# Recurrent gates on TensorE: one product for both neighbour tiles, from a tile that DMAs assemble

## The chip, the cores and the metric

The kernel runs on one core of a Trainium2 chip. The time is that of the device in microseconds; the kernel before took 1741.39 us (median of three runs, 1741.05 to 1741.88).

## What is computed

Two networks in a row on 256 tokens of width 1024: two layers with feed-forward blocks, a recurrent mixer (layer 0) or a pooling mixer (layer 1) and an embedding gate, then two layers with attention and a gated linear recurrence. The change touches only the gates of the recurrent mixer:

```python
xc = conv_b + sum(conv_w[k] * shifted(xb, k))            # 256 tokens x 1280 channels
xh = xc.reshape(B, S, 16, 80)                            # 16 heads of 80 channels
r  = sigmoid(einsum('bshi,hij->bshj', xh, w_a) + b_a)    # each head has its own 80 x 80 matrix
ig = sigmoid(einsum('bshi,hij->bshj', xh, w_x) + b_x)
a  = exp(-8 * r * softplus(-a_param))
h  = scan of a * h + sqrt(1 - a*a) * (ig * xc);  y = h * gelu(gate_branch);  out = y @ w_out
```

## The kernel before

It is one program with a hand-written order on each engine. Weights come in 1 MB blocks on SyncE's queue (L286) into a ring of three; ScalarE copies each block to its rounded part `hi` (L455), VectorE makes the rest `lo` (L927), and TensorE multiplies with both. This "split" of a block stands at the head of each iteration of a stage on ScalarE and VectorE, two blocks ahead of TensorE.

The recurrent mixer ("lru") has ten iterations of input projection, i = 0 to 9. In i = 0 to 4 TensorE makes the recurrent branch, two tiles of 128 channels each time. VectorE takes them out of PSUM (L1396) and convolves them (`convolve`, two instructions of L1406 and six of L1410 for two tiles); each tile that is finished adds 1 to `xc_ready`. So tiles 0 to 9 of `xc` exist in pairs, tiles 8 and 9 last.

The gates come in two groups, g = 0 and 1, of five tiles (640 channels, eight heads) each. Heads of 80 don't end where tiles of 128 end, so an output tile m of a group takes input from tiles m - 1, m and m + 1. `band` holds the heads' matrices as 128 x 128 blocks around the diagonal, zero elsewhere: 2 gates x 2 groups x 5 tiles x 384 columns. POOL clears it at the start (L337) and 48 small DMAs fill it (L356). For each output tile and each gate, TensorE makes two fp32 products at the ends of a group and three inside it (L2168), 13 for each group and gate. Group 0 follows the projection of i = 5 (called `half`), group 1 that of i = 6. Before a group TensorE waits for all of its five tiles of `xc`.

Both gates of the tile `ft` (0 to 9) go to bank `ft % 4` of psD. ScalarE applies the two sigmoids to it (L672, L673), each of which adds 1 to `gates_ready`, and from ft = 4 on TensorE waits until the bank's last reader is done: `gates_ready >= 2 * (ft - 3)` (L2164). So ft = 4 wants both sigmoids of ft = 0, and ft = 9 those of ft = 5.

ScalarE's order around this is, for i = 5: split of block 7, sigmoids of group 0, tanh of group 0 (L680); for i = 6: split of block 8, exp (L686) and sqrt (L688) of group 0, gelu of the first four gate tiles (L693), sigmoids of group 1; for i = 7: the next split, tanh of group 1 and so on. A function of another set than the last one needs a table load ahead of it, which has the line of its activation. The waits of `split` beyond one are semaphore instructions of their own (L449).

Of the kernel before, what the change touches and what calls it, by code (L numbers as in the profile page):

```python
# [25 lines left out]
P = 128  # L26
S = 256
# [4 lines left out]
R = 1280  # L32
RT = R // P
HD = 80
GT = 5
# [26 lines left out]
L_XC = L_XB + RT * (S + 3) + 2  # L62
L_GELU = L_XC + RT * S
L_IG = L_GELU + RT * S
BAND = L_IG + RT * S
POOL_M, POOL_B, POOL_S = 4096, 6144, 7168
Z, Q_B, V_B, A_QK, A_V, G_B, GATE_A, GATE_B = 2048, 4096, 5120, 6144, 8192, 9216, 10240, 12288
LOGF, TMP, KK = 14336, 16384, 18432
# [4 lines left out]
QK_T = GATE_B  # L73
SQUARES, TURNER = 22016, 22528
SCRATCH = 22784
assert BAND + 2 * 2 * GT * 384 <= SCRATCH


def head_pieces():
# [12 lines left out]
def build(nc, a, out):  # L92
# [5 lines left out]
    def sem(name):  # L98
        return ctx.enter_context(nc.semaphore(name))

    with ctx:
# [12 lines left out]
        scr = sb("scr", [P, SCRATCH])  # L114
# [13 lines left out]
        psD = ctx.enter_context(nc.psum_tensor("psD", [P, 4, 512], F32))  # L128
# [20 lines left out]
        first_landed, early_landed = sem("first_landed"), [sem(f"early_landed{i}") for i in range(2)]  # L149
        consts_loaded, gain_loaded = sem("consts_loaded"), sem("gain_loaded")  # L150
        band_zeroed, band_loaded = sem("band_zeroed"), sem("band_loaded")
        p_loaded, pool_loaded, mix_loaded = sem("p_loaded"), sem("pool_loaded"), sem("mix_loaded")
        param_loaded, param_turned = sem("param_loaded"), sem("param_turned")
        ident_loaded, first_gain_loaded, gains_loaded, gains_turned, gains_ready = sem("ident_loaded"), sem("first_gain_loaded"), sem("gains_loaded"), sem("gains_turned"), sem("gains_ready")
# [178 lines left out]

        @block.gpsimd
        def _(pool):
            band = view(BAND, 2, 2, GT, 384)
            pool.memset(scr[:, BAND:BAND + 2 * 2 * GT * 384], 0.0).then_inc(band_zeroed, 1)  # L337
            pool.dma_start(param_rows[0:4 * RT, :], a["lru_conv_w"][0].rearrange("k (f p) -> (k f) p", p=P)).then_inc(param_loaded, 16)
            for i, v in enumerate((a["lru_conv_b"], a["lru_b_a"], a["lru_b_x"], a["lru_a_param"])):
                pool.dma_start(param_rows[(4 + i) * RT:(5 + i) * RT, :], v[0].rearrange("(f p) -> f p", p=P)).then_inc(param_loaded, 16)  # L340
            for l in range(2):
                for e in range(2):
                    at = 8 * RT + (2 * l + e) * HEADS
                    pool.dma_start(param_rows[at:at + HEADS, :], a["hg_lb_logits_2"][e, l, :].rearrange("(f p) -> f p", p=P)).then_inc(param_loaded, 16)
            for i, g in enumerate(gains[1:]):
                pool.dma_start(gain_rows[1][i * KT:(i + 1) * KT, :], g.rearrange("(k p) -> k p", p=P)).then_inc(gains_loaded, 16)
            for t_, src in ((level_words, a["c_level"]), (rope_in[:], a["c_freq"]),
                            (pos_i[:], a["positions_2"].rearrange("b (t p) -> p (b t)", p=P))):
                pool.dma_start(t_, src, allow_slow_non_contiguous=True).then_inc(consts_loaded, 16)
            pool.wait_ge(band_zeroed, 1)  # L350
            pool.wait_ge(hi_ready, RAW + 2)
            for m, w in enumerate((a["lru_w_a"][0], a["lru_w_x"][0])):
                for head, row, tile, part, cnt in head_pieces():
                    col = head * HD - (tile - 1) * P
                    for g in range(2):
                        pool.dma_start(band[part:part + cnt, m, g, tile, col:col + HD],  # L356
                                       w[8 * g + head, row:row + cnt, :]).then_inc(band_loaded, 16)
            if row_gains:
                pool.dma_start(gain[:], row_gains[0].rearrange("(o d) -> o d", o=1).broadcast_to([P, D])).then_inc(gain_loaded, 16)
            rescaled = updates = 0  # L360
            for stage, nxt in zip(plan, plan[1:] + [("end",)]):
                kind = stage[0]
                if kind == "renorm":

                    pool.wait_ge(gain_loaded, 16 * (rescaled + 1))
                    for i, (t, c) in enumerate(BY_COLUMNS):
                        pool.wait_ge(h_ready, 2 * T * updates + i + 1)
                        cs = slice(512 * c, 512 * (c + 1))
                        pool.tensor_tensor(xn[:, t, cs], h[:, t, cs], gain[:, cs], ALU.mult).then_inc(hg_ready, 1)
                    rescaled += 1  # L370
                    if rescaled < len(row_gains):
                        pool.wait_ge(hg_ready, 2 * T * rescaled)
                        pool.dma_start(gain[:], row_gains[rescaled].rearrange("(o d) -> o d", o=1).broadcast_to([P, D])).then_inc(gain_loaded, 16)
                if kind == "pool":

                    pool.wait_ge(pool_loaded, 48)
                    pool.tensor_tensor(view(POOL_B, D), view(POOL_B, D), view(POOL_S, D), ALU.mult).then_inc(rows_biased, 1)
                if kind in ("ffn", "lru", "pool", "ple", "mix", "renorm", "rescale"):
                    updates += 1
                if kind == "lru":  # L380
                    pool.wait_ge(h_ready, 2 * T * (updates + 1))
                    pool.dma_start(view(POOL_M, T, 4, S), a["c_pool"]).then_inc(pool_loaded, 16)
                    pool.dma_start(view(POOL_B, D), a["pool_b"].broadcast_to([P, D])).then_inc(pool_loaded, 16)
                    pool.dma_start(view(POOL_S, D), a["pool_scale"].broadcast_to([P, D])).then_inc(pool_loaded, 16)
                if kind == "lru" or kind == "ple" and stage[2] == 0:
                    i = 0 if kind == "lru" else 1
                    pool.wait_ge(h_ready, 2 * T * (updates + 1))
                    pool.dma_start(view(PTOK, T, S), a["p"][i].rearrange("b (t p) d -> p (b t) d", p=P)).then_inc(p_loaded, 16)
                if kind == "lru" or kind == "mix" and stage[1] == 0:
                    l = 0 if kind == "lru" else 1  # L390
                    pool.wait_ge(h_ready, 2 * T * (updates + 1))
                    pool.dma_start(view(NRM_DA, 512), a["da_norm_2"][l].rearrange("(o d) -> o d", o=1).broadcast_to([P, 512])).then_inc(mix_loaded, 16)
                    pool.dma_start(view(NRM_HG, 512), a["hg_norm_2"][l].rearrange("(o d) -> o d", o=1).broadcast_to([P, 512])).then_inc(mix_loaded, 16)
                    pool.dma_start(view(LAM, 256), a["da_lambda_2"][l].rearrange("(o i) d -> o (i d)", o=1).broadcast_to([P, 256])).then_inc(mix_loaded, 16)
# [36 lines left out]
        def _(act):  # L431
# [133 lines left out]
            for stage, nxt in zip(plan, plan[1:] + [("end",)]):  # L565
# [98 lines left out]
                if kind == "lru":  # L664
                    half = R // FC
                    gelu = view(L_GELU, RT, S)
                    r, ig, th = view(L_R, RT, S), view(L_IG, RT, S), view(L_XB, RT, S)

                    def recurrent_gates(g):
                        for ft in range(g * GT, (g + 1) * GT):  # L670
                            act.wait_ge(gates_done, ft + 1)
                            act.activation(r[:, ft, :], psD[:, ft % 4, 0:S], ACT.Sigmoid, bias=lru_c[:, 1, ft:ft + 1]).then_inc(gates_ready, 1)  # L672
                            act.activation(ig[:, ft, :], psD[:, ft % 4, S:2 * S], ACT.Sigmoid, bias=lru_c[:, 2, ft:ft + 1]).then_inc(gates_ready, 1)  # L673
# [21 lines left out]
                    for i in range(2 * half):  # L695
# [6 lines left out]
                            recurrent_decay(1)  # L702
                        n += 1
                        if i == half:
                            recurrent_gates(0)
                            half_tanh(0)
                        if i == half + 1:
                            recurrent_decay(0)
# [1057 lines left out]
        def _(pe):  # L1766
# [293 lines left out]
            for stage, nxt in zip(plan, plan[1:] + [("end",)]):  # L2060
# [92 lines left out]
                    st["ffn"] += 1  # L2153
                if kind == "lru":
                    half = R // FC
                    band, xc = view(BAND, 2, 2, GT, 384), view(L_XC, RT, S)

                    def recurrent_gates(g):

                        pe.wait_ge(xc_ready, GT * (g + 1))  # L2160
                        for m in range(GT):
                            ft = g * GT + m
                            if ft >= 4:
                                pe.wait_ge(gates_ready, 2 * (ft - 3))  # L2164
                            for e in range(2):
                                ks = [k for k in (m - 1, m, m + 1) if 0 <= k < GT]
                                for k in ks:
                                    last = pe.matmul(psD[:, ft % 4, e * S:(e + 1) * S], band[:, e, g, k, (m - k + 1) * P:(m - k + 2) * P],  # L2168
                                                     xc[:, g * GT + k, :], start=(k == ks[0]), stop=(k == ks[-1]))
                            last.then_inc(gates_done, 1)  # L2170

                    for i in range(2 * half):
# [240 lines left out]
```

## Time and profile before

| | |
|---|---|
| median of the runs | 1741.39 us |
| profiled execution, time | 1741.45 us |
| profiled execution, span | 1739.6 us |
| TensorE busy (matmuls) | 1728.8 us, 99% |
| VectorE busy | 1262.9 us, 73% |
| ScalarE busy | 1003.7 us, 58% |
| DMA | 311.65 MB, mean 179 GB/s |

The span is the time from the first to the last instruction of the profiled execution; its time is measured around it. Busy shares are means over the whole span and over stages with different limits, so a change in a stretch of 30 us is read in the rows of that stretch. All times in the timelines are microseconds from the start of the span. The recurrent gates lie between 231 and 260 us.

### The profile page before, as it was taken

The numbers are of one execution on the slowest core, as the hardware profiler recorded it, in microseconds if no ns is written. First come the engines' busy times: TensorE is split into PE (matmuls) and PEld (weight loads), VectorE is DVE, ScalarE is ACT, GpSimd is POOL, SyncE is SP. The second block draws the span as 40 slices with busy tenths as digits, with TensorE's granted clock in tenths as the row PEclk, the third lists the DMA queues.
The fourth block names the chain that finished last, engine by engine and source line by source line (L and its number), as shares of the span: only waits on it lengthen the run. The fifth ranks groups of instructions, "written<-read, shape, count | busy, mean of one in ns | idle before, by whom it ended". The sixth has DMA issues, their size and how long they took to land.

```text
span 1739.6 us, 24239 instructions
## 1 busy us (share of the span) xinstructions
PE 1728.8 (99%) x9535; PEld 1500.2 (86%) x9535; DVE 1262.9 (73%) x1602; ACT 1003.7 (58%) x1247; POOL 58.9 (3%) x95
## 2 busy tenths in 40 slices
PE   9999999999999999999999999999999999999998
PEld 8888998888888888888889888888888988888887
DVE  6766777766677666876667898867666898876665
ACT  7544566654467444754457866464446966565444
POOL 7200000000000000000001000000000000000000
PEclk9999999999999999999999999999999999999999
DMA  7755435665545655465545544356555554446552
GB/s 244 255 189 188 162 122 170 217 222 189 191 169 181 212 187 176 144 208 185 189 145 194 184 165 145 122 186 220 190 192 170 163 176 134 138 165 215 188 186 88
DMA packets 211564, 311.65 MB, mean 179 GB/s; under 512 B 6434, under 2 KB 166112, under 8 KB 211360
## 3 DMA queue, kind: packets, MB, share of 16 engines
q1 hardware_dynamic: 207472, 303.84, 53.4%
q0 software_dynamic: 3712, 6.44, 1.2%
q8 instruction: 50, 0.82, 0.2%
q10 hardware_dynamic: 304, 0.33, 0.1%
q14 instruction: 26, 0.21, 0.0%
HBM read 309.54 MB, written 1.05 MB: 179 GB/s over the span
## 4 chain that ended last, share of the span: by engine, by line
PE 91%; ACT 4%; DVE 3%; issue 1%; DMA 0%; SPq 0%; DVEq 0%; ACTq 0%
PE psD L1945 28%; PE psA L1834 27%; PE psA L1839 14%; PE psA L1912 3%; PE psA L1927 3%; PE psA L1778 3%; PE psA L1945 2%; PE psD L2231 2%; PE psA L1931 1%; PE psA L1916 1%; PE psA L1783 1%; PE psA L2015 1%; ACT hi L455 1%; PE psD L2168 1%; PE psD L2015 1%
## 5 line engine op out<-in xcount | busy, mean ns | idle before, releaser
L927 DVE TENSOR_TENSOR lo<-raw,hi 128x2048 fp32r<-128x2048 f32 x285 | 650.5, 2290 | 171.9 <-ACT hi L455 171.2
L455 ACT ACTIVATE hi<-raw 128x2048 fp32r<-128x2048 f32 x285 | 542.4, 1909 | 77.2 <-PE psD L1945 33.5
L1834 PE MATMUL psA<-xT,hi 128*128 128x512 f32 x2094 | 501.1, 390 | 0.1
L1834 PEld LDWEIGHTS psA<-xT,hi 128*128 128x128 f32 x2094 | 387.2, 188 | 77.0 <-DVE xT L960 0.3
L1839 PEld LDWEIGHTS psA<-xT,lo 128*128 128x128 f32 x2112 | 271.9, 191 | 11.8 <-issue 0.5
L1839 PE MATMUL psA<-xT,lo 128*128 128x256 f32 x2112 | 276.8, 283 | 0.1
L1945 PE MATMUL psD<-hi,prod_hi 128*128 128x512 f32 x544 | 213.4, 392 | 0.0
L1945 PE MATMUL psD<-hi,prod_lo 128*128 128x512 f32 x544 | 212.6, 391 | 0.0
L1945 PE MATMUL psD<-lo,prod_hi 128*128 128x512 f32 x544 | 143.6, 389 | 0.0
L593 ACT ACTIVATE scr<-psA 128x512 f32<-128x512 f32 x66 | 39.3, 595 | 163.3 <-PE psA L1839 163.3
L608 ACT ACTIVATE prod_hi<-scr 128x512 fp32r<-128x512 f32 x66 | 41.7, 632 | 157.8 <-DVE scr L1309 157.8
L1945 PEld LDWEIGHTS psD<-lo,prod_hi 128*128 128x128 f32 x544 | 102.1, 188 | 21.3
L1945 PEld LDWEIGHTS psD<-hi,prod_lo 128*128 128x128 f32 x544 | 102.4, 188 | 19.4
L1945 PEld LDWEIGHTS psD<-hi,prod_hi 128*128 128x128 f32 x544 | 102.4, 188 | 19.4
L598 ACT ACTIVATE scr<-psA 128x512 f32<-128x512 f32 x66 | 39.2, 594 | 132.7 <-PE psA L1839 132.7
L1945 PE MATMUL psD<-hi,xT 128*128 128x512 f32 x368 | 101.9, 393 | 0.0
L1303 DVE TENSOR_TENSOR scr<-psA,scr 128x512 f32<-128x512 f32 x66 | 45.6, 690 | 76.1 <-ACT scr L598 76.1
L1292 DVE TENSOR_TENSOR scr<-psA,scr 128x512 f32<-128x512 f32 x66 | 45.5, 689 | 71.4 <-ACT scr L593 71.4
L1778 PE MATMUL psA<-xT,hi 128*128 128x256 f32 x704 | 89.9, 284 | 0.0
L1778 PEld LDWEIGHTS psA<-xT,hi 128*128 128x128 f32 x704 | 86.5, 191 | 0.1
L1311 DVE TENSOR_TENSOR prod_lo<-scr,prod_hi 128x512 fp32r<-128x512 f32 x66 | 45.7, 692 | 46.7 <-ACT prod_hi L608 46.7
L1945 PEld LDWEIGHTS psD<-hi,xT 128*128 128x128 f32 x368 | 67.9, 188 | 13.4
(308 smaller groups left out, 1926.2 us busy)
## 6 DMA issues: line engine op xcount, KB each, us to landing
raw<-in_w_in SPq DMA_DIRECT2D x48, 1024.0 KB, 5.2
raw<-in_ffn_w_up SPq DMA_DIRECT2D x43, 1024.0 KB, 5.4
raw<-in_ffn_w_gate SPq DMA_DIRECT2D x43, 1024.0 KB, 5.4
raw<-in_ffn_w_down SPq DMA_DIRECT2D x43, 1024.0 KB, 5.0
raw<-in_w_gate SPq DMA_DIRECT2D x22, 1024.0 KB, 5.3
raw<-in_w_up SPq DMA_DIRECT2D x22, 1024.0 KB, 5.3
raw<-in_w_down SPq DMA_DIRECT2D x22, 1024.0 KB, 4.9
raw<-in_lru_w_in SPq DMA_DIRECT2D x10, 1024.0 KB, 5.3
```

Of the source, the lines that this page charges most:

```text
L455: act.activation(hi[:, n % RING, :], raw_of(n), ACT.Copy).then_inc(hi_ready, 1)
L608: act.activation(span(prod_hi[:, c % 2]), prod[:, c % 2, :], ACT.Copy).then_inc(prod_hi_ready, 1)
L927: dve.tensor_tensor(lo[:, n % RING, :], raw_of(n), hi[:, n % RING, :].bitcast(F32), ALU.subtract).then_inc(lo_ready, 1)
L1292: dve.tensor_tensor(both(sil[:, c % 2, :]), psA[:, 0:2, 0:S], gate_l, ALU.add).then_inc(gate_summed, 1)
L1303: dve.tensor_tensor(up[:, c % 2], psA[:, 2:4, 0:S], up_l, ALU.add).then_inc(up_summed, 1)
L1311: dve.tensor_tensor(span(prod_lo[:, c % 2]), prod[:, c % 2, :], span(prod_hi[:, c % 2]).bitcast(F32), ALU.subtract).then_inc(prod_lo_ready, 1)
L1778: pe.matmul(to[:, f * S:(f + 1) * S], w_hi[:, k, f * P:(f + 1) * P], x[:, k, :], start=(begin and f == 0 and k == 0 and x is xTh), stop=False)
L1834: pe.matmul(psA[:, bank + f, :], w_hi[:, k, f * P:(f + 1) * P], xT[:, k].rearrange("p e s -> p (e s)"), start=(k == 0), stop=False)
L1839: last = pe.matmul(psA[:, bank + f, 0:S], w_lo[:, k, f * P:(f + 1) * P], xTh[:, k, :], start=(begin and k == 0), stop=(k == KT - 1))
L1912: pe.matmul(psA[:, t, :], x[:, k, t * P:(t + 1) * P], w_hi[:, k, :], start=(k == 0 and x is xTh), stop=False)
L1927: pe.matmul(psA[:, t, :], x[:, KT // 2 + k, t * P:(t + 1) * P], w_hi[:, k, :], start=False, stop=False)
L1945: last = pe.matmul(to[:, 2 * t + c, :], x[:, k, ts], w[:, k, half_of[c]], start=(first and k == 0 and e == 0), stop=(final and k == 1 and ...
```

## The change

`band` now holds, for each gate and group, two sets of 640 columns: set 0 has the rows that come from even tiles, set 1 those from odd tiles. For an output tile m, the set `m % 2` has the rows of tile m itself, and the other set has in rows 64 to 127 what comes from tile m - 1 and in rows 0 to 63 what comes from tile m + 1 (a head reaches at most 64 rows into a neighbour). The new area `cross` has for each inner tile (m = 1 to 3) one tile with rows 64 to 127 of tile m - 1 and rows 0 to 63 of tile m + 1. So each output tile takes two products for each gate: its own tile, and the neighbour (at the ends of a group) or the cross tile.

The cross tiles are assembled by DMAs on ScalarE's queue, in four calls of `cross_rows(g, part)` with two DMAs each, from SBUF to SBUF. Part 0 makes the cross tiles of m = 1 and 2 (64 partitions x 2 KB for each DMA), part 1 that of m = 3 (64 x 1 KB). Three of the calls, (0, 0), (0, 1) and (1, 0), stand ahead of the sigmoids of group 0 on ScalarE; (1, 1) stands between these and the tanh. Each call waits until the convolution has finished the last tile that it reads: `xc_ready` of 4, 5, 9 and 10. TensorE waits for the landing of a part at m = 1 and m = 3, and for `xc_ready` tile by tile instead of once for a group. The order of the groups among the other work stays.

```diff
--- before.py
+++ after.py
@@ -63,6 +63,7 @@
 L_GELU = L_XC + RT * S
 L_IG = L_GELU + RT * S
 BAND = L_IG + RT * S
+CROSS = BAND + 2 * 2 * 2 * R // 2
 POOL_M, POOL_B, POOL_S = 4096, 6144, 7168
 Z, Q_B, V_B, A_QK, A_V, G_B, GATE_A, GATE_B = 2048, 4096, 5120, 6144, 8192, 9216, 10240, 12288
 LOGF, TMP, KK = 14336, 16384, 18432
@@ -73,7 +74,7 @@
 QK_T = GATE_B
 SQUARES, TURNER = 22016, 22528
 SCRATCH = 22784
-assert BAND + 2 * 2 * GT * 384 <= SCRATCH
+assert CROSS + 2 * 3 * S <= SCRATCH
 
 
 def head_pieces():
@@ -149,6 +150,7 @@
         first_landed, early_landed = sem("first_landed"), [sem(f"early_landed{i}") for i in range(2)]
         consts_loaded, gain_loaded = sem("consts_loaded"), sem("gain_loaded")
         band_zeroed, band_loaded = sem("band_zeroed"), sem("band_loaded")
+        cross_landed = [[sem(f"cross_landed{g}{part}") for part in range(2)] for g in range(2)]
         p_loaded, pool_loaded, mix_loaded = sem("p_loaded"), sem("pool_loaded"), sem("mix_loaded")
         param_loaded, param_turned = sem("param_loaded"), sem("param_turned")
         ident_loaded, first_gain_loaded, gains_loaded, gains_turned, gains_ready = sem("ident_loaded"), sem("first_gain_loaded"), sem("gains_loaded"), sem("gains_turned"), sem("gains_ready")
@@ -333,8 +335,8 @@
 
         @block.gpsimd
         def _(pool):
-            band = view(BAND, 2, 2, GT, 384)
-            pool.memset(scr[:, BAND:BAND + 2 * 2 * GT * 384], 0.0).then_inc(band_zeroed, 1)
+            band = view(BAND, 2, 2, 2, GT * P)
+            pool.memset(scr[:, BAND:CROSS], 0.0).then_inc(band_zeroed, 1)
             pool.dma_start(param_rows[0:4 * RT, :], a["lru_conv_w"][0].rearrange("k (f p) -> (k f) p", p=P)).then_inc(param_loaded, 16)
             for i, v in enumerate((a["lru_conv_b"], a["lru_b_a"], a["lru_b_x"], a["lru_a_param"])):
                 pool.dma_start(param_rows[(4 + i) * RT:(5 + i) * RT, :], v[0].rearrange("(f p) -> f p", p=P)).then_inc(param_loaded, 16)
@@ -351,9 +353,8 @@
             pool.wait_ge(hi_ready, RAW + 2)
             for m, w in enumerate((a["lru_w_a"][0], a["lru_w_x"][0])):
                 for head, row, tile, part, cnt in head_pieces():
-                    col = head * HD - (tile - 1) * P
                     for g in range(2):
-                        pool.dma_start(band[part:part + cnt, m, g, tile, col:col + HD],
+                        pool.dma_start(band[part:part + cnt, m, g, tile % 2, head * HD:(head + 1) * HD],
                                        w[8 * g + head, row:row + cnt, :]).then_inc(band_loaded, 16)
             if row_gains:
                 pool.dma_start(gain[:], row_gains[0].rearrange("(o d) -> o d", o=1).broadcast_to([P, D])).then_inc(gain_loaded, 16)
@@ -666,6 +667,15 @@
                     gelu = view(L_GELU, RT, S)
                     r, ig, th = view(L_R, RT, S), view(L_IG, RT, S), view(L_XB, RT, S)
 
+                    xc, cross = view(L_XC, RT, S), view(CROSS, 2, 3, S)
+
+                    def cross_rows(g, part):
+
+                        k0, k1 = ((0, 2), (2, 3))[part]
+                        act.wait_ge(xc_ready, GT * g + k1 + 2)
+                        act.dma_start(cross[P // 2:P, g, k0:k1, :], xc[P // 2:P, g * GT + k0:g * GT + k1, :]).then_inc(cross_landed[g][part], 16)
+                        act.dma_start(cross[0:P // 2, g, k0:k1, :], xc[0:P // 2, g * GT + k0 + 2:g * GT + k1 + 2, :]).then_inc(cross_landed[g][part], 16)
+
                     def recurrent_gates(g):
                         for ft in range(g * GT, (g + 1) * GT):
                             act.wait_ge(gates_done, ft + 1)
@@ -702,7 +712,11 @@
                             recurrent_decay(1)
                         n += 1
                         if i == half:
+                            cross_rows(0, 0)
+                            cross_rows(0, 1)
+                            cross_rows(1, 0)
                             recurrent_gates(0)
+                            cross_rows(1, 1)
                             half_tanh(0)
                         if i == half + 1:
                             recurrent_decay(0)
@@ -2153,20 +2167,25 @@
                     st["ffn"] += 1
                 if kind == "lru":
                     half = R // FC
-                    band, xc = view(BAND, 2, 2, GT, 384), view(L_XC, RT, S)
+                    band, xc, cross = view(BAND, 2, 2, 2, GT * P), view(L_XC, RT, S), view(CROSS, 2, 3, S)
 
                     def recurrent_gates(g):
 
-                        pe.wait_ge(xc_ready, GT * (g + 1))
                         for m in range(GT):
                             ft = g * GT + m
+                            pe.wait_ge(xc_ready, GT * g + min(m + 2, GT))
                             if ft >= 4:
                                 pe.wait_ge(gates_ready, 2 * (ft - 3))
+                            if 0 < m < GT - 1:
+                                pe.wait_ge(cross_landed[g][m // 3], 32)
+                                beside = cross[:, g, m - 1, :]
+                            else:
+                                beside = xc[:, g * GT + (1 if m == 0 else m - 1), :]
+                            ms = slice(m * P, (m + 1) * P)
                             for e in range(2):
-                                ks = [k for k in (m - 1, m, m + 1) if 0 <= k < GT]
-                                for k in ks:
-                                    last = pe.matmul(psD[:, ft % 4, e * S:(e + 1) * S], band[:, e, g, k, (m - k + 1) * P:(m - k + 2) * P],
-                                                     xc[:, g * GT + k, :], start=(k == ks[0]), stop=(k == ks[-1]))
+                                bank = psD[:, ft % 4, e * S:(e + 1) * S]
+                                pe.matmul(bank, band[:, e, g, m % 2, ms], xc[:, ft, :], start=True, stop=False)
+                                last = pe.matmul(bank, band[:, e, g, (m + 1) % 2, ms], beside, start=False, stop=True)
                             last.then_inc(gates_done, 1)
 
                     for i in range(2 * half):
```

## Rows read from the trace of the kernel before

**Rows 1.** The page: busy time by engine, granted clock, chain that ended last.

```profile
PE 1728.8 (99%) x9535; PEld 1500.2 (86%) x9535; DVE 1262.9 (73%) x1602; ACT 1003.7 (58%) x1247; POOL 58.9 (3%) x95
...
PEclk9999999999999999999999999999999999999999
...
PE 91%; ACT 4%; DVE 3%; issue 1%; DMA 0%; SPq 0%; DVEq 0%; ACTq 0%
```

**Rows 2.** Line L2168: its instructions; duration ns min/median/max.

```profile
L2168 PE MATMUL psD<-scr x104: 377/379/483, 231.0 to 259.4; 128*128 128x256 f32 x104
```

**Rows 3.** Chain of waits, 200 to 290 us: start us, us, what.

```profile
207.66 0.45 PE psD L2039 x4
...
231.15 11.24 PE psD L2168 x52
...
242.41 0.47 ACT scr L672
...
257.41 0.37 ACT scr L673
...
257.83 1.99 PE psD L2168 x8
```

**Rows 4.** Timeline of ScalarE, 205 to 285 us: start us, us, instruction.

```profile
226.19 1.92 ACT L455 ACTIVATE hi<-raw 128x2048 fp32r<-128x2048 f32 x1 [4.54 <-DMA raw<-in_lru_w_in]
228.13 1.28 ACT L672 ACT_TABLE_LOAD   x1
232.92 0.47 ACT L672 ACTIVATE scr<-psD,lru_c 128x256 f32<-128x256 f32 x1 [3.51 <-PE psD L2168]
233.29 0.47 ACT L673 ACTIVATE scr<-psD,lru_c 128x256 f32<-128x256 f32 x1
...
243.34 2.11 ACT L680 ACTIVATE scr<-scr,cpos 128x256 f32<-128x256 f32 x5
245.36 1.90 ACT L455 ACTIVATE hi<-raw 128x2048 fp32r<-128x2048 f32 x1
247.27 1.28 ACT L686 ACT_TABLE_LOAD   x1
248.57 2.10 ACT L686 ACTIVATE scr<-scr,cpos 128x256 f32<-128x256 f32 x5
```

**Rows 5.** Timeline of TensorE, same stretch.

```profile
257.83 1.99 PE L2168 MATMUL psD<-scr 128*128 128x256 f32 x8 [0.21 <-ACT scr L673]
```

**Rows 6.** VectorE: timelines, and busy time of PE, PEld, DVE, ACT, POOL.

```profile
222.56 2.71 DVE L1410 SCALAR_TENSOR_TENSOR scr<-scr,conv_w 128x256 f32<-128x256 f32 x6
...
237.04 0.88 DVE L1410 SCALAR_TENSOR_TENSOR scr<-scr,conv_w 128x256 f32<-128x256 f32 x2
...
219.00:237.50 18.50, 18.50 (x133) 17.73 (x132) 18.07 (x30) 6.80 (x7) 0.00 (x0) 1.00 0.47 157
```

**Rows 7.** Timeline of all engines, 0.5 to 4 us.

```profile
1.40 0.36 ACTq L541 DMA_DIRECT2D ident<-in_c_ident  x1
...
1.79 1.28 ACT L543 ACT_TABLE_LOAD   x1 [1.79 <-issue]
```

**Rows 8.** Line L449, 242 to 244 us: its instructions.

```profile
L449 ACTq EVENT_SEMAPHORE  x1: 17/17/17, 243.5 to 243.5; - x1
```

**Rows 9.** DMA issues by line: KB each, us from issue to landing.

```profile
raw<-in_lru_w_in SPq DMA_DIRECT2D x10, 1024.0 KB, 5.3
...
scr<-in_pool_scale POOLq DMA_DIRECT2D x1, 512.0 KB, 7.3
...
out<-scr ACTq DMA_DIRECT2D x1, 256.0 KB, 2.6
```

**Rows 10.** Timelines of POOL and TensorE at the start; TensorE's longest wait.

```profile
0.75 6.50 POOL L337 MEMSET scr<- 128x7680 f32 x1 [0.29 <-POOLq L2403]
...
1.14 4.21 PE L2054 MATMUL psD<-one_row 128*128 128x128 f32 x18 [1.14 <-DVE one_row L1131]
...
PE psD L2054 <- DVE one_row L1131: 1.1, 1, 1.1
```

## Prediction

> **What bounds the kernel now.** I read the page first. TensorE is busy for 99% of the span at a granted clock that never falls, and the chain that ended last is TensorE for 91% [rows 1]. A kernel so full gets faster only where TensorE time leaves the path. Then I looked at the line that the change touches, L2168: 104 passes, since each fp32 product shows as two, so 52 products [rows 2]. By the chain of waits, 52 passes of the first group follow each other in 11.24 us, 0.216 us a pass [rows 3]. (The 379 ns of one row is modelled and overlaps its neighbours; the chain's 0.216 is what a pass costs.) The change leaves 10 products for 13 in each of the four pairs of group and gate, so 12 products, 24 passes, 24 x 0.216 = 5.19 us less. That is the whole possible gain, 0.30%.
>
> Whether it arrives must be read from the two places. The chain from 231.15 us is: first group on TensorE to 242.39; then **ScalarE alone** from 242.41 to 257.78 (last sigmoids of the group, tanh, a split, exp, sqrt, gelu, each with its table load, first two sigmoids of the second group); then TensorE's last 8 passes [rows 3, 4]. So the first group is on the path. Of the second group only the last tile (ft=9) is: its bank was that of ft=5, it waits until both sigmoids of ft=5 are done, and the timeline shows TensorE resuming at 257.83 with 0.21 us idle before it [rows 5]. TensorE's other 44 passes there ran beside ScalarE with just that little to spare.
>
> **The second group.** It loses 12 passes, 12 x 0.216 = 2.59 us, all of them in ft=6 to 8, ahead of that wait. ScalarE's stretch doesn't depend on them: after the first group it waits for nothing until 257.78 (its rows follow each other without idle time [rows 4]). What was 0.21 us of idle time becomes some 2.8 us, and the gain here is 0. The next thing that is late is the same wait as before.
>
> **The first group.** It too loses 12 passes, 2.59 us, and that would move ScalarE's stretch forward. But the change puts DMA issues into ScalarE's stream ahead of the group's sigmoids, and the third pair of them, cross_rows(1, 0), waits for xc_ready 9, that is for tile 8 of the convolution. Behind that wait in ScalarE's stream stand the table load and all sigmoids of the first group, and TensorE needs the sigmoids of ft=0 before it may start ft=4 (L2164). So step by step:
> - Tile 8 is finished by the fifth instruction of the last six of L1410, which begins at 237.04 and takes 0.48 us: 237.52 [rows 6]. VectorE is busy for 18.07 of the 18.50 us from 219 to there [rows 6], with no wait among them, and nothing that feeds it moves, so this time stands.
> - Two DMA issues on ScalarE's queue. The issue of ident took 0.36 us [rows 7], so 0.72: 238.29 with some 0.05 for the semaphore.
> - The sigmoids' table load, 1.28 us. Before, it ran at 228.13, hidden under the wait for TensorE's first tile [rows 4]. It now follows the issues, since in these rows each load stands directly ahead of the activation that needs it [rows 4]: at the start of the kernel it comes at 1.79, after the two issues, not before them [rows 7]. First sigmoid at 239.6.
> - The two sigmoids of ft=0: from 232.92, and 0.47 from 233.29 [rows 4], 0.84 us: 240.44.
> - TensorE has done ft=0 to 3 in 32 passes by 231.15 + 6.91 = 238.06, and stands idle 2.4 us. It resumes 0.05 after the sigmoid, as at 257.83 after 257.78: 240.49. The 8 passes of ft=4 take 1.99 with their latency, as at 257.83 to 259.82 [rows 3, 5]: 242.48.
> - ScalarE meanwhile works off ft=0 to 3, eight sigmoids at 0.37 us (232.92 to 233.29) [rows 4], and is ready for ft=4 at 239.6 + 8 x 0.37 = 242.5. So ft=4's begin at 242.5 where before they began at 242.41: **+0.1 us**. Two limits meet there, and nothing is left of the 2.59.
>
> **The last pair of issues**, cross_rows(1, 1), stands between the sigmoids of the first group and the tanh. If its 0.72 us begins when the last sigmoid ends, it is all on the path. But ScalarE's sequencer runs ahead of its engine: the semaphore instruction of L449, which stands behind the five tanh, ran at 243.5, while the engine was at the first of them (243.34) and the split behind it began at 245.36 [rows 4, 8]. The issue can then run from 242.55 to 243.3, under the two sigmoids of ft=4. Bounds 0 and +0.72; I take 0, by that row. The first two pairs are issued in the same way under the split of 226.19 (tile 4 was ready at 225.2 [rows 6]), from 226.3 to 227.7, at no cost.
>
> **Landing.** No copy between two places of SBUF is in the trace. The nearest rows are ScalarE's 256 KB store, 2.6 us, and under load 5.3 us (1 MB of weights) and 7.3 us (a broadcast row of pool_scale) [rows 9]. A pair is 256 KB or less. (0, 0) is issued by 227.0 and lands between 229.6 and 234.3. It is wanted for ft=1 at 232.9: a stall of 0 to 1.4 us, all of it inside the 2.4 us for which TensorE waits at ft=4 anyway. So the price is 0 unless landing takes over 8 us. (1, 0), issued by 238.3, is wanted at 250; (1, 1) at 253.4. Both have at least as much time. I take 0; the other bound is some +1.
>
> **The rest, with one answer.** TensorE's added waits (xc_ready tile by tile, the landings) gate nothing but what stands above. The band's DMAs are 48 as before and wait, as before, for an early split of ScalarE. POOL's memset shrinks from 7,680 to 5,120 columns, 6.50 to 4.33 us by proportion [rows 10]; the small loads behind it start 2.2 us earlier, among the first weight loads, one of which the start of the kernel waits for. That may cost or give 0.3 us; I take 0. No code after the gates changes, and every engine there moves by the same shift.
>
> **Sum.** 0 (second group) + 0.1 (first group) + 0 (last issues) + 0 (landing, start) = +0.1 us on the profiled execution, whose span is 1739.6 and whose time is 1741.45, beside the median of 1741.39. I put the forecast at 1741.5: no change.
>
> A page speaks of the price of the table load. The Trainium skill (ScalarE: Activation LUTs, What ACT_TABLE_LOAD costs) adds to 1283 ns a drain of about 1380 ns for a switch of sets. The rows here show the load starting within 0.02 us of the split's end and exp 0.02 us after the load (247.27, 248.57) [rows 4], so no drain is in them. By the page the first group would end 1.4 us later and the sum would be +1.5.
>
> **Rivals.** *The saved passes count in full.* For it: TensorE is on the path in [rows 1]. Against it: both waits above. It needs sigmoids at 233 and a ScalarE stretch that is shorter by 2.6. It gives 1741.4 - 5.2 = 1736.2. Chance 0.03.
>
> *The table load keeps its place ahead of the issues.* Then the first sigmoid starts at 238.3, TensorE resumes at 239.2, ft=4 is ready at 241.2 for 242.41: -1.2 us, 1740.2. Against it: the order at the start [rows 7]. Chance 0.06.
>
> *The issues aren't hidden or a landing is late.* +0.7 to +1.7 us, 1742.1 to 1743.1. Chance 0.16.
>
> *TensorE's clock falls in the new gaps* (the rival on the slow side). The kernel before has no wait over 1.1 us on TensorE [rows 10], and its granted clock holds at 1.00, which is 2.4 GHz [rows 6]. The change makes two gaps, of 2.4 and 2.8 us. The rows that show a slow clock are the first ones, when the engine had done nothing before: 18 passes of 128 columns in 4.21 us, 0.234 each, where later four such took 0.45, 0.112 each [rows 3, 10]. The ratio is that of 1.2 to 2.4 GHz, though the granted clock has no fall there. Such a stretch loses about 2.2 us. After the second gap it would lie straight on the path: +2.3, 1743.7. If the first gap does it too, the 8 passes of ft=4 double, +1.7 more: 1745.5 in all. It decides as soon as the granted clock falls ahead of 258 us. The Trainium skill (TensorE: Matmul & The Clock Gate, Why this matters for your kernels) warns that an idle gap between bursts of matmuls can put the clock back to its lower level; no row of this kernel shows such a fall, and by the rule the sum would be +2.3. Chance 0.10, of which 0.06 is for both gaps.
>
> **How the numbers follow.** Forecast 0.65, within half a microsecond of 1741.5. The range takes in the table-load rival, the unhidden issues and the fall after one gap, each with the 0.4 us by which the runs differ: 1739.6 to 1744.2. It leaves out the full gain and the fall after both gaps, about 0.1, and what I haven't thought of. A measurement of this kernel can tell about 0.2%, 3.5 us, from no change. Faster by more than that is the first rival with a little for surprises, 0.04; slower is the fall after both gaps and surprises, 0.07; the same 0.89.
>
> **What would show it.** In the profile after: 80 passes on L2168, not 104; the table load of L672 at 238.3, not 228.1; the first sigmoid near 239.6; TensorE idle some 2.4 us ahead of ft=4 and 2.8 us ahead of ft=9, both put down to L673; the first tanh within 0.8 us of 243.4; ft=9 resumed near 257.9. The forecast is wrong if the first sigmoid comes near 233, if TensorE waits for a landing longer than for L673, or if the granted clock shows less than 1.00 between 238 and 270.

## The result, and the profile after

The changed kernel takes 1745.12 us (median of 16 runs, 1742.04 to 1746.55), the kernel before 1741.07 (16 runs, 1740.57 to 1741.88). The ratio is 1.002, with a 95% interval of 1.0014 to 1.0027: slower by about 4 us, just over the 0.2% that the prediction calls a change. It lies above the range of 1739.6 to 1744.2.

Two things stand out. The runs spread over 4.5 us where those of before spread over 1.3. And each run reports TensorE's mean granted clock: 0.999 or 1.0 in all runs of before whose clocks are listed, but 0.998 or less in 13 of these 16. The three at 0.999 took 1742.5 on average, the others 1744.5 to 1746.0 by their clock. The profiled execution is one of the three, the fastest: 1742.04, span 1740.2. So its trace shows the path, and not what happens in most executions. The page of it, as [rows 1]:

```profile
PE 1722.7 (99%) x9511; PEld 1494.4 (86%) x9511; DVE 1263.0 (73%) x1602; ACT 1004.1 (58%) x1247; POOL 57.1 (3%) x95
...
PEclk9999999999999999999999999999999999999999
...
PE 88%; ACT 5%; DVE 5%; issue 2%; DMA 0%; ACTq 0%; SPq 0%; DVEq 0%
```

Line L2168 has become two lines; 40 passes each, 80 for the 104 of [rows 2]:

```profile
L2187 PE MATMUL psD<-scr x40: 377/379/455, 230.5 to 259.4; 128*128 128x256 f32 x40
...
L2188 PE MATMUL psD<-scr x40: 378/379/379, 230.9 to 259.9; 128*128 128x256 f32 x40
```

ScalarE around the gates, as [rows 4]; columns are start, duration, instruction, and in brackets the idle time ahead of it:

```profile
225.85 0.53 ACTq L676 DMA_DIRECT2D scr<-scr  x1
226.41 0.61 ACTq L677 DMA_DIRECT2D scr<-scr  x1
...
237.04 0.47 ACTq L676 DMA_DIRECT2D scr<-scr  x1
237.54 0.62 ACTq L677 DMA_DIRECT2D scr<-scr  x1
238.19 1.28 ACT L682 ACT_TABLE_LOAD   x1 [10.43 <-DVE scr L1424]
239.49 0.47 ACT L682 ACTIVATE scr<-psD,lru_c 128x256 f32<-128x256 f32 x1
...
242.47 0.48 ACT L682 ACTIVATE scr<-psD,lru_c 128x256 f32<-128x256 f32 x1
242.48 0.47 ACTq L676 DMA_DIRECT2D scr<-scr  x1
...
242.98 0.62 ACTq L677 DMA_DIRECT2D scr<-scr  x1
243.70 2.11 ACT L690 ACTIVATE scr<-scr,cpos 128x256 f32<-128x256 f32 x5 [0.39 <-ACT scr L683]
...
257.67 0.47 ACT L683 ACTIVATE scr<-psD,lru_c 128x256 f32<-128x256 f32 x1
```

The reader should see three things. The first four issues ran at 225.85 to 228.3, beside the split of 225.84 to 227.8, and though the last of them outlasts it by 0.6 us, nothing behind them was ready to run, so they cost nothing, as forecast. The third pair waited until 237.04, and behind it came the table load and the first sigmoid, at 239.49, where before it came at 232.92. And the last pair ran ahead of the engine (it starts at 242.48, with the sigmoid of ft=4), but with 1.1 us it is longer than the two sigmoids that cover it, so the first tanh waits until 243.70. The chain of waits shows both places, VectorE's last instruction for tile 8 to the issue, and 0.29 us of the last issue by itself:

```profile
236.53 0.89 DVE scr L1424 x2
237.42 0.09 ACTq L676
...
243.31 0.29 ACTq L677
```

TensorE, as [rows 5], with its two new gaps in brackets:

```profile
240.47 0.67 PE L2187 MATMUL psD<-scr 128*128 128x256 f32 x2 [2.94 <-ACT scr L683]
...
258.28 0.67 PE L2187 MATMUL psD<-scr 128*128 128x256 f32 x2 [3.19 <-ACT scr L683]
```

The copies land in 2.3 to 5.5 us (the page gives medians for each size), and TensorE nowhere waits for one:

```profile
scr<-scr ACTq DMA_DIRECT2D x4, 128.0 KB, 2.3
...
scr<-scr ACTq DMA_DIRECT2D x4, 64.0 KB, 4.4
```

Counted from the first pass of the gates (230.99 before, 230.47 after; the start of the kernel differs from execution to execution), TensorE resumes at ft=9 26.84 us later before and 27.81 later after. **The path is 0.97 us longer**, where the forecast has 0.1. With the start 0.52 us earlier that makes 1741.45 + 0.97 - 0.52 = 1741.9, for the 1742.04 of this execution. The other 3 us of the median aren't in this trace.

### The profile page after: what moved, and what is told of

Read it like the earlier page. It is cut to its first block, busy times and chain, and to the rows that moved or that the text cites. A ratio compares the mean times of both kernels' runs of the same rounds, so it can differ in the third digit from the quotient of the medians.

```text
span 1740.2 us, 24207 instructions
## 1 busy us (share of the span) xinstructions
PE 1722.7 (99%) x9511; PEld 1494.4 (86%) x9511; DVE 1263.0 (73%) x1602; ACT 1004.1 (58%) x1247; POOL 57.1 (3%) x95
## 4 chain that ended last, share of the span: by engine, by line
PE 88%; ACT 5%; DVE 5%; issue 2%; DMA 0%; ACTq 0%; SPq 0%; DVEq 0%
PE psD L1959 28%; PE psA L1848 27%; PE psA L1853 14%; PE psA L1926 3%; PE psA L1941 3%; PE psA L1959 2%; PE psD L2250 2%; PE psA L1945 1%; PE psA L1930 1%; PE psA L1792 1%; ACT hi L456 1%; PE psA L2029 1%; DVE scr L1424 1%; PE psA L1797 1%; DVE lo L941 1%
```

## Experiments

**Theory:** the two gaps of 2.9 and 3.2 us let TensorE's clock fall in most executions (the fourth rival of the prediction), and ScalarE's issues lengthen the path. **Rival:** something about the copies varies, landing times or ScalarE's issues. Each kernel of an experiment was timed in 11 runs (pool_inner9 in 9) beside 21 to 33 of the kernel before on the same chip, whose median was 1741.16 to 1741.36. In the table, "gaps" is TensorE's wait ahead of ft=4 and of ft=9 by the profile, and "low clock" the number of runs with a mean granted clock of 0.998 or less. A fall of the size found below, some 3.4 us at half the clock, takes 0.001 off the mean of 1740 us (an estimate from those rows), so the count can miss one: fill_first's median run, 1743.68, reports 0.999.

| kernel | gaps, us | median | lowest to highest | low clock |
|---|---|---|---|---|
| before | 0, 0.2 | 1741.07 | 1740.57 to 1741.88 | none |
| changed, 16 runs | 2.9, 3.2 | 1745.12 | 1742.04 to 1746.55 | 13 of 16 |
| again | 2.9, 3.2 | 1745.04 | 1741.93 to 1746.94 | 10 of 11 |
| fill_first | 0.4, 3.2 | 1743.68 | 1741.84 to 1745.76 | 9 of 11 |
| fill_second | 2.9, 0.6 | 1743.10 | 1742.02 to 1744.99 | 6 of 11 |
| fill_both | 0.4, 0.6 | 1742.12 | 1741.48 to 1742.93 | 0 of 11 |
| before_gap2 | 0, 2.8 | 1742.13 | 1740.40 to 1743.97 | 6 of 11 |
| before_gap_long | 0, 5.4 | 1743.54 | 1742.41 to 1744.26 | 11 of 11 |
| fill_tanh_first | 0.3, 0.4 | 1742.10 | 1741.39 to 1742.73 | 0 of 11 |
| pool_fill | 0, 0.3 | 1741.55 | 1740.24 to 1742.31 | 0 of 11 |
| pool_issue | 0, 2.9 | 1740.05 | 1738.21 to 1741.80 | 7 of 11 |
| before_inner9 | 0, 0 | 1741.78 | 1741.04 to 1742.83 | 0 of 11 |
| act_inner9 | 2.9, 0 | 1741.62 | 1739.34 to 1743.11 | 6 of 11 |
| pool_inner9 | 0, 0 | 1736.21 | 1735.75 to 1737.35 | 0 of 9 |

### The changed kernel again

> The changed kernel once more, to see whether its times spread and where TensorE's clock falls. Clock theory (the two gaps of 2.9 and 3.2 us that the change makes ahead of ft=4 and ft=9 put TensorE's granted clock down in some executions): times between 1742 and 1747, far more spread than the 1.3 us of the kernel before, and each slow one with a lower mean clock (0.996 to 0.998 for 0.999); a profile of such an execution shows the granted clock below 1.00 right behind the first or second gap. Rival (something else than the clock varies, such as the landing of the cross tiles or of the first loads): the slow executions show a wait for a DMA on TensorE, ScalarE or VectorE and a clock of 1.00 throughout.

The spread came back, and this profiled execution (1744.65 us) shows what the first one could not. Stretches of TensorE; columns are the stretch, its length, busy time (instructions), granted clock, DMA share, GB/s:

```profile
256.00:259.40 3.40, 0.33 (x2) 1.00 0.00 0
...
260.90:263.00 2.10, 2.10 (x10) 0.50 0.00 0
263.00:264.00 1.00, 1.00 (x6) 0.50 0.00 0
264.00:266.00 2.00, 2.00 (x18) 0.92 0.03 8
266.00:268.00 2.00, 2.00 (x19) 1.00 0.02 6
```

After the gap ahead of ft=9 the clock is at 1.00 for a while, then at 0.50, which is 1.2 GHz, from about 260.9 until about 264.3 (the mean of 0.92 from 264 to 266 has the last 0.3 us of it), and back. The timeline shows the passes of that stretch:

```profile
259.52 0.67 PE L2187 MATMUL psD<-scr 128*128 128x256 f32 x2 [3.19 <-ACT scr L683]
...
260.89 1.03 PE L2188 MATMUL psD<-scr 128*128 128x256 f32 x2
261.36 5.50 PE L1792 MATMUL psA<-xT,hi 128*128 128x256 f32 x32
266.70 2.08 PE L1797 MATMUL psA<-xT,lo 128*128 128x256 f32 x16
268.62 4.00 PE L1792 MATMUL psA<-xT,hi 128*128 128x256 f32 x32
```

From the resumption at ft=9 to the next projection it takes 268.62 - 259.52 = 9.10 us, for 265.83 - 258.28 = 7.55 in the execution without a fall: 1.55 us, all on the path. This execution also started 1.2 us later, which the start of the kernel does by itself (TensorE there waited 0.9 us for the input x). No engine waits for a copy.

### Closing the gaps

```diff
+                                if 0 < m < GT - 1:          # fill_first: and g == 0; fill_second: and g == 1
+                                    pe.matmul(bank, band[:, e, g, m % 2, ms], xc[:, ft, :], start=True, stop=True)
                                 pe.matmul(bank, band[:, e, g, m % 2, ms], xc[:, ft, :], start=True, stop=False)
```

> The changed kernel with the own-tile product of the inner output tiles made twice (the first result is overwritten), so 104 passes as before: the DMAs, the order on ScalarE and the path through ScalarE stay, only the gaps close to some 0.4 and 0.6 us. Clock theory: 1742.0, spread of about 1 us as the kernel before has. Rival (DMA landings or ScalarE's issues cause the slow executions): 1745 with the spread of the changed kernel.

> The same filling in the first group only: the gap ahead of ft=4 closes to 0.4 us, that of 3.2 us ahead of ft=9 stays. Clock theory, if the second gap alone does it: 1744 to 1745. If each gap does its part: about 1743.5. If the first gap does it: 1742.0. Rival (not the clock): 1745.

> The changed kernel with the own-tile product of the inner tiles made twice in the second group only: the gap of 2.9 us ahead of ft=4 stays, that of 3.2 us ahead of ft=9 closes to 0.6 us. With both closed the time was 1742.12, with the first closed 1743.68, with none 1745.04. Clock theory with each gap on its own: 1742.12 + 1745.04 - 1743.68 = 1743.5, spread 1742 to 1746, the fall at 242 to 246. Rival (the second gap alone does it and the first only adds to the chance there): 1742.1.

More work on TensorE makes the kernel faster: with both gaps filled, 1742.12 and a spread of 1.5 us, no low clock in 11 runs; with none, 1745.04. The ratio to the kernel before is 1.0006 (0.9997 to 1.0015) for the one and 1.002 (1.0011 to 1.0029) for the other. The copies, their issues on ScalarE and their order are the same in all four kernels, and they land in like times (medians of 2.3 to 2.6 us for 128 KB, 3.9 to 4.5 us for 64 KB), so the rival falls. The path stays too: in fill_both ft=9 starts 27.82 us after the first pass of the gates (259.13 - 231.31), for the 27.81 of the changed kernel. What is left of the waits for ScalarE in fill_both (two, the longer one 0.6 us; columns are total, times, longest):

```profile
PE psD L2189 <- ACT scr L683: 1.0, 2, 0.6
```

One gap open costs 1.6 us (the second) or 1.0 us (the first) over fill_both, both 2.9. As times these steps are no larger than their uncertainty (the intervals of the ratios are 0.0009 to either side, 1.6 us), but the low clocks, 9 and 6 of 11 for none, show that each gap does its part. The profiled execution of fill_first shows its fall behind the second gap. The first two passes take 1.19 us, where they took 0.67:

```profile
259.39 1.19 PE L2189 MATMUL psD<-scr 128*128 128x256 f32 x2 [3.19 <-ACT scr L683]
...
257.00:260.00 3.00, 0.61 (x2) 0.85 0.00 0
260.00:262.00 2.00, 2.00 (x6) 0.50 0.00 0
262.00:264.00 2.00, 2.00 (x14) 0.87 0.04 8
```

That of fill_second caught none; the fall behind the first gap stands in act_inner9's, below.

### Gaps in the kernel before, without a copy

```diff
                                 ks = [k for k in (m - 1, m, m + 1) if 0 <= k < GT]
+                                if g == 1 and len(ks) == 3:
+                                    ks = ks[:2]        # before_gap_long: ks = [m]
```

> The kernel before with one product less for the inner tiles of the second group (the input from the next tile is left out, so those gates miss a part): 12 passes fewer there, no DMAs, no other order. It makes a gap of some 2.8 us ahead of ft=9 and nothing else. The path says 1741.1, no change. Clock theory: 1741.1 in some executions and up to 4 us more in others. Rival (DMAs or issues): 1741.1 in all.

> The kernel before with both neighbour products of the inner tiles of the second group left out (those gates miss two parts): 24 passes fewer, so the gap ahead of ft=9 is some 5.4 us, twice that of the kernel with 12 fewer, which took 1742.13 (1740.4 to 1744.0). The path says 1741.1. Clock theory: the fall comes in all or nearly all executions and costs some 2.2 us or more, median 1743 to 1744. Rival (the spread comes from something that the gap's length doesn't touch): 1742.1 again.

The path of these kernels is that of the kernel before: in both, ft=9 starts 26.83 us after the first pass of the gates, for 26.84 (the profiled execution of before_gap2 caught no fall). And yet their medians are 1.0 and 2.4 us longer: 12 passes fewer cost 1.0 us, 24 fewer cost 2.4 (ratio 1.0015, 1.0006 to 1.0024; the first, 1.0007, 0.9998 to 1.0016, can't be told from none by its ratio, though its spread and 6 low clocks can). With the gap twice as long, all 11 runs have a low clock. Its profiled execution, the 8 passes of ft=9 in 3.78 us for 1.99 [rows 5]:

```profile
257.25 3.78 PE L2170 MATMUL psD<-scr 128*128 128x256 f32 x8 [5.39 <-ACT scr L673]
...
255.00:258.00 3.00, 0.75 (x2) 0.72 0.00 0
258.00:260.00 2.00, 2.00 (x7) 0.50 0.00 0
260.00:262.00 2.00, 2.00 (x9) 0.50 0.00 0
262.00:264.00 2.00, 2.00 (x14) 0.71 0.00 0
264.00:266.00 2.00, 2.00 (x19) 1.00 0.03 8
```

### The issues on ScalarE

```diff
 # fill_tanh_first: the changed kernel with both gaps filled, and
                             recurrent_gates(0)
-                            cross_rows(1, 1)
                             half_tanh(0)
+                            cross_rows(1, 1)
 # pool_fill: both gaps filled, and the eight DMAs in POOL's stream for "lru"
+                    for g in range(2):
+                        for part, (k0, k1) in enumerate(((0, 2), (2, 3))):
+                            pool.wait_ge(xc_ready, GT * g + k1 + 2)
+                            pool.dma_start(...)   # the two copies of cross_rows
```

> The changed kernel with both gaps filled (1742.12), and the last pair of issues moved behind the tanh of the first group. In the changed kernel's profile the first tanh starts 0.39 us late, behind the issues. If that is on the path, as the profile says: 1742.12 - 0.4 = 1741.7, and the split behind starts right after the tanh. Rival (the issues only move their delay on to the split, or the landing comes late for ft=8): 1742.1.

> The DMAs of the cross tiles on POOL's queue, and the own-tile product of all inner tiles made twice, so TensorE has as many passes as before and no gap. It measures what the DMAs, their landings, the finer waits and the shorter memset cost by themselves. Theory (only ScalarE's stream pays for the copies): 1741.2, as the kernel before. Rival (the copies or the start of the kernel cost something wherever they are issued): 1741.7 or more, for the 1742.12 that the same kernel takes with the issues on ScalarE.

pool_fill takes 1741.55, beside 1741.36 for the kernel before on that chip (ratio 1.0002, 0.9992 to 1.0011): copies, finer waits and the shorter memset cost nothing that the times can show. Its trace shows 0.09 us: TensorE resumes at ft=9 0.14 us after the sigmoid's end, for 0.05 in the kernel before, and so 26.93 us after the first pass for 26.84. The changed kernel has the same 0.14. With the issues on ScalarE the same work took 1742.12 beside 1741.16. The 0.8 us between is of the size of the 0.88 that the trace gives to ScalarE's stretch (below).

The expectation of fill_tanh_first missed: 1742.10, not 1741.7. Its profile shows the issue under the tanh, which starts 0.08 us after the sigmoids' end:

```profile
244.08 0.51 ACT L690 ACTIVATE scr<-scr,cpos 128x256 f32<-128x256 f32 x1
244.22 0.47 ACTq L676 DMA_DIRECT2D scr<-scr  x1
```

From the first pass of the gates to the end of the sigmoids of ft=5 it has 0.3 us less than fill_both (258.52 - 231.14 = 27.38 for 258.99 - 231.31 = 27.68). The medians, each against its own runs of before (+0.74 and +0.96), agree with 0.2 of it, but their intervals are 0.0009, 1.6 us, to either side, so the times alone settle nothing. The traces do: before the change the first tanh also started 0.09 us after the sigmoids (242.78 + 0.47, 243.34), so of the 0.39 only 0.30 is due to the issues, and 0.30 is what fill_tanh_first gains.

### Taking the gain

pool_issue moves the eight DMAs to POOL and fills nothing. pool_inner9 also moves ft=9 of the second group into the projection of i=7, between the products with `hi` and those with `lo`:

```diff
                     high(0, 0, KT)
                     high(1, 0, KT)
+                    if between:
+                        between()      # for i == half + 2: recurrent_gates(1, (GT - 1,))
                     pe.wait_ge(lo_ready, n_at)
...
                         if i == half + 1:
-                            recurrent_gates(1)
+                            recurrent_gates(1, range(GT - 1))
```

> The changed kernel with the eight DMAs of the cross tiles issued on POOL's queue, where nothing waits, and so not ahead of the sigmoids on ScalarE. Theory of the path (ScalarE's issues and the wait for tile 8 took the first group's gain): the first sigmoid comes 1.9 us after the group's start as before, the first group gives its 2.59 us, the last pair of issues costs nothing; ahead of ft=9 a gap of some 2.8 us stays. Lowest time 1738.5, median some 1740 with the clock's part of one gap. Rival (landings set the first group's pace, whoever issues): a wait for the landing on TensorE at ft=1 or ft=3, time of 1741 or more.

> As with POOL's queue, and the last tile of the second group (ft=9) moved into the projection of i=7, between its products with hi and those with lo, so that TensorE has 3.8 us of work while ScalarE reaches the sigmoids of ft=5. Theory: no gap is left, all 24 passes are saved on TensorE (5.19 us) and ScalarE's stretch comes 2.6 us earlier, which the pieces of y behind it, 2.8 us ahead of need before, can bear: 1741.1 - 5.2 = 1736.0, spread of 1 us. Rival (ScalarE's or VectorE's chain to the y pieces becomes the bound): 1737 to 1738.5, with a wait of TensorE for xT near 285.

Both came close to what was expected. The four runs of pool_issue with a clock of 0.999 took 1738.56 on average, 2.6 us under the median of before: the first group's 2.59 us arrive once nothing stands ahead of its sigmoids. The one gap left takes more than half of that back (1.5 us) in the median of 1740.05 (ratio 0.9992, 0.9983 to 1.0001). pool_inner9 takes 1736.21 us, ratio 0.9973 (0.9963 to 0.9983), 5 us faster than the kernel before: nearly all of both groups' 5.19 us arrives, and without a gap the clock stays: no low clock in nine runs, with the same 80 passes and the same copies as pool_issue, which has one in 7 of 11. So it is the gap and not the smaller number of passes that lowers the clock. In its profile the first sigmoid is back at 232.46, TensorE waits only 0.63 us for the y pieces at 282.50, and POOL issues the copies that waited for tile 8:

```profile
232.46 0.47 ACT L680 ACTIVATE scr<-psD,lru_c 128x256 f32<-128x256 f32 x1 [3.26 <-PE psD L2184]
...
282.50 3.96 PE L1955 MATMUL psD<-hi,xT 128*128 128x512 f32 x16 [0.63 <-DVE xT L964]
...
237.38 0.52 POOL L369 DMA_DIRECT2D scr<-scr  x1 [11.62 <-DVE scr L1418]
```

> The kernel before with nothing changed but the place of ft=9, moved into the projection of i=7. It tells whether the gain of the version with POOL's queue and this move (1736.2) comes from the move or from the fewer passes. Theory (the move only makes room for what the fewer passes save, and the kernel before has 0.21 us of idle time there): 1741.0. Rival (the move is itself the gain): 1738 or less.

> The changed kernel, issues on ScalarE as they are, with ft=9 moved into the projection of i=7. Theory: the second group's 2.59 us arrive on TensorE and its gap is gone; the first group's gap of 2.9 us stays, with some 0.6 us of lateness and its part of the clock, about 1 us; ScalarE's stretch is still 1 us late, so TensorE waits 1 us for the y pieces. Lowest time 1741.1 + 0.6 - 2.6 + 1.0 = 1740.1, median 1741, with a spread over 2 us and falls behind the first gap only. Rival (only the move counts, ScalarE's issues don't matter): 1736.2.

The move alone gains nothing: 1741.78, above the 1741.0 expected (ratio 1.0002, 0.9993 to 1.0011); its profile has waits of 0.7 us for VectorE and 0.6 for the y pieces in place of the 0.2 at ft=9. So the 5 us come with the fewer passes, and not with the move. The move without POOL's queue has 1741.62 for the 1741 expected, and 1739.99 on average in the five runs at 0.999. Its profiled execution catches the fall behind the first gap, which ends at 241.52. It reaches ft=4's passes only in part, so that their first sigmoid, at 244.10, waits 0.54 us for TensorE:

```profile
242.00:244.00 2.00, 2.00 (x8) 0.69 0.76 281
244.00:246.00 2.00, 2.00 (x12) 0.50 0.72 259
246.00:248.00 2.00, 2.00 (x18) 0.96 0.14 28
```

That sigmoid comes 12.57 us after the first pass of the gates (244.10 - 231.53), for 12.00 in the changed kernel's execution without a fall. From ft=4 to the second group TensorE loses 1.54 us (250.62 - 241.52 = 9.10 for 248.03 - 240.47 = 7.56), but only the 0.57 reaches ScalarE's stretch. In the changed kernel the rest would end in the gap ahead of ft=9. A fall behind the second gap has nothing of the kind behind it. That fits a first gap that costs less than the second, though it is read from one execution.

## Why the prediction was wrong

**Right, by its steps.** 80 passes for 104. The second group's passes turn into idle time ahead of ft=9 (forecast 2.8, found 3.2). The first group's gain is lost to the wait for tile 8 that now stands ahead of the sigmoids: idle 2.9 us ahead of ft=4 for 2.4. The table load follows the issues (238.19 for 238.3) and the first sigmoid comes at 239.49 for 239.6, absolute times that hide the earlier start of this execution. The landings were no matter, and neither were the band and the memset. No drain is seen around a table load in the profile after either: the split ends at 247.62, the load starts at 247.64, takes 1.28 us, and exp starts at 248.93, as in [rows 4]. So the trace doesn't agree with the drain of about 1380 ns that the Trainium skill (ScalarE: Activation LUTs, What ACT_TABLE_LOAD costs) adds.

**Mis-sized, two terms of the sum.** Two issues were put at 2 x 0.36 us by the row of ident [rows 7]. A pair of these copies takes 0.47 + 0.62 us. The view that [rows 7] is taken from has a longer issue on the same queue just above, which the prediction passed over:

```profile
0.76 0.61 ACTq L540 DMA_DIRECT2D scr<-in_ffn_norm  x1
```

The longer pair makes the first sigmoid 0.4 us later than forecast, and TensorE's slower resumption ahead of ft=4 (0.14 us after the sigmoid, not 0.05) adds 0.1. So the sigmoids of ft=4 come 12.00 us after the gates' start (242.47 - 230.47) for 11.42 before: +0.58 for +0.1. And "the last pair: bounds 0 and +0.72, I take 0" was +0.30: the sequencer did run ahead, but the pair of issues is longer than its cover. With 0.09 for the slower resumption at ft=9 that is +0.97. By itself this would have given 1742.1, inside the range.

**Failed: the sum has no term for TensorE's clock.** The step that failed is the price of nothing for the two new gaps, with a chance of 0.06 for a fall behind both. Low clocks came in 13 of 16 runs, and the clock costs 2.9 us of the median. The prediction had the mechanism and its place as a rival. The argument against it was that "no row of this kernel shows such a fall". But the kernel before has no wait over 1.1 us after which one could have been seen [rows 10], so its trace was silent, not against. The one thing that did speak was the page of the Trainium skill (TensorE: Matmul & The Clock Gate, Why this matters for your kernels), and the runs agree with its warning: a gap of 2.8 to 3.2 us lowers the clock in a part of the executions, one of 5.4 us in all 11, waits up to 0.7 us in none of 53.

That the rival's 1745.5 is so near the 1745.12 measured is partly luck. It has 3.9 us for the clock, 2.2 and 1.7, where the runs have 2.9, and 0.1 for the path, where they have 1.0. What a fall takes of TensorE's time is 1.5 us in each of the four profiled executions that have one behind a gap of 2.9 to 3.2 us (again, fill_first, pool_issue, act_inner9), and 2.8 us behind 5.4 (10.36 us from ft=9 to the next projection, for 7.57). Why one execution is spared and another not is open.

The sum that the runs support is then 1741.1 + 1.0 (path; fill_both) + 2.9 (clock in both gaps; again over fill_both) = 1745.0.

## What to carry to other kernels

Work taken from an engine that is busy for 99% can be worth nothing, as here, where its next step waits for another engine; find that wait first, and move what stands behind it, as pool_inner9 does. Ask of each gap that an edit opens on TensorE what the clock will do, and give it a real chance even if the trace of before shows no fall, since it has no gap. And put a DMA that waits for a late producer on a queue where nothing stands behind it.

## What the runs showed of the hardware

- The fall and the gap can stand apart. In `again` the clock fell 1.4 us after TensorE had resumed (259.5, 260.9), in act_inner9 1.2 us after (241.5, 242.8). In fill_first and pool_issue it fell 0.3 us ahead of the resumption, and the very first passes after the gap are slow. In these four it stayed down for some 3.4 us. With the gap of 5.4 us it was already down when TensorE resumed at 257.25 (mean of 0.72 from 255 to 258), and stayed so until about 263.2, for some 6.8 us.
- Filling both gaps with products that nobody uses, 24 passes more, made the changed kernel 2.9 us faster.
- A DMA issue on ScalarE's queue takes 0.47 to 0.62 us for a copy of 64 partitions within SBUF, for 0.36 us with the load of ident and 0.61 with that of ffn_norm; on POOL's queue 0.52. The copies of 64 and 128 KB that ScalarE issued landed in 2.3 to 5.5 us in the changed kernel.
- ScalarE's sequencer issues a DMA while its engine still works on the activation ahead (225.85 under the split of 225.84), and the last pair, which starts under the sigmoids of ft=4, delays the tanh only by what outlasts them.
